# First expert pair gathered straight into its operand, low halves on GpSimd, gate/up weights in halves, last three pairs unpipelined, 32-bit down weights

## What is computed

```python
g_sel = argmax(x @ w_rg + b_rg)                 # one group of 4
e_prob = softmax(e_logits of that group)        # 8 experts
top_v, top_i = top_k(e_prob, 2)                 # two of them, weights normalised
h = silu(x @ w_gate[e]) * (x @ w_up[e])         # 1024 -> 256
y += (h * gate[e]) @ w_down[e]                  # 256 -> 1024
```

## Time and profile before

| | |
|---|---|
| median of 3 runs | 1422.86 us (1418.54 to 1423.76) |
| profiled execution | 1424.52 us, span 1423.2 us |
| PE busy | 1260.6 us (89%) |
| DVE busy | 713.2 us (50%) |
| ACT busy | 511.3 us (36%) |
| GpSimd busy | 141.6 us (10%) |
| moved by DMA | 340.32 MB, mean 239 GB/s |
| mean granted TensorE clock | 0.937 |

### The profile page before, as it was taken

The page is one execution under the profiler, slowest core; times in us unless marked ns, Lnnn a source line. Parts: engine busy times, 40 slices in busy tenths (PEclk is TensorE's granted clock), DMA queues, the critical chain, the costliest instruction groups (busy, mean ns, idle before and its releaser), DMA issues. The chain is left out here.

```text
span 1423.2 us, 21723 instructions
## 1 busy us (share of the span) xinstructions
PE 1260.6 (89%) x8724; PEld 791.9 (56%) x8724; DVE 713.2 (50%) x1273; ACT 511.3 (36%) x839; POOL 141.6 (10%) x185
## 2 busy tenths in 40 slices
PE   6799999989888789988989998969897969998885
PEld 5676678866665543433336766756664734333332
DVE  3655376655434514645465665436433451564553
ACT  3443323154332213343345333454432311433433
POOL 5100031110000101101001130000000101110100
PEclk9899998799998789999999998999998989999998
DMA  8464353357648049999973468503873616999992
GB/s 240 155 210 129 114 159 115 109 167 283 234 163 332 35 194 388 422 420 421 421 288 114 144 205 311 178 1 104 313 262 151 262 71 239 420 421 421 421 421 108
DMA packets 112835, 340.32 MB, mean 239 GB/s; under 512 B 7487, under 2 KB 75403, under 8 KB 84049
## 3 DMA queue, kind: packets, MB, share of 16 engines
q1 hardware_dynamic: 107296, 322.20, 60.4%
q0 software_dynamic: 4992, 15.47, 3.5%
q10 hardware_dynamic: 432, 1.11, 0.2%
HBM read 328.21 MB, written 10.54 MB: 238 GB/s over the span
## 5 line engine op out<-in xcount | busy, mean ns | idle before, releaser
L2151 PE MATMUL ps<-arena,mkv 128*64 128x512 f32 x1024 | 240.3, 623 | 36.6 <-DMA arena<-in_w_exp_up 27.6
L558 PE MATMUL ps<-bx,wh 128*128 128x320 f16 (+1 forms) x640 | 194.5, 304 | 32.8 <-DVE wl L552 10.6
L552 DVE SCALAR_TENSOR_TENSOR wl<-stg,wh 128x1024 f16<-128x1024 f32 x128 | 160.9, 1296 | 96.1 <-ACT wh L545 95.9
L559 PE MATMUL ps<-bx,wh 128*128 128x320 f16 (+1 forms) x640 | 194.4, 304 | 0.0
L560 PE MATMUL ps<-bx,wl 128*128 128x320 f16 (+1 forms) x640 | 194.1, 303 | 0.0
L545 ACT ACTIVATE wh<-stg 128x1024 f16<-128x1024 f32 x128 | 128.4, 1050 | 177.5 <-PE ps L560 154.5
L2151 PEld LDWEIGHTS ps<-arena,mkv 128*64 128x64 f32 x1024 | 87.4, 143 | 175.6 <-issue 175.2
L2367 DVE SCALAR_TENSOR_TENSOR wl<-arena,wh 128x1024 f16<-128x1024 f32 x56 | 67.6, 1248 | 63.9 <-ACT wh L2315 63.9
L558 PEld LDWEIGHTS ps<-bx,wh 128*128 128x128 f16 x640 | 64.9, 101 | 59.1 <-issue 27.5
L558 PE MATMUL ps<-arena,wh 128*128 128x320 f16 x288 | 88.3, 307 | 3.7 <-DVE arena L1381 3.0
L559 PE MATMUL ps<-arena,wh 128*128 128x320 f16 x288 | 88.2, 306 | 0.0
(11 more groups left out here) (440 smaller groups left out, 1962.7 us busy)
## 6 DMA issues: line engine op xcount, KB each, us to landing
arena<-in_w_exp_gate SPq DMA_DIRECT2D x64, 1024.0 KB, 15.0
arena<-in_w_exp_up SPq DMA_DIRECT2D x64, 1024.0 KB, 17.1
arena<-in_w_exp_down SPq DMA_DIRECT2D x32, 1024.0 KB, 19.8
stg<-in_w_exp_down SPq DMA_DIRECT2D x32, 1024.0 KB, 18.0
arena<-in_cache_mem_k SPq DMA_DIRECT2D x16, 1024.0 KB, 7.2
arena<-in_cache_mem_v SPq DMA_DIRECT2D x16, 1024.0 KB, 4.9
stg<-in_w_in_a SPq DMA_DIRECT2D x28, 512.0 KB, 4.7
stg<-in_w_qkv_c SPq DMA_DIRECT2D x20, 512.0 KB, 4.6
```

The source lines that it names most:

```text
L552: nc.vector.scalar_tensor_tensor(wl[:, s, c], src[:, c], WSCALE, wh[:, s, c], ALU.mult, ALU.subtract).then_inc(S["w_lo"], 1)
L558: nc.tensor.matmul(out, wh[:, s, at:at + 128], hi, start=start, stop=False)
L559: nc.tensor.matmul(out, wh[:, s, at:at + 128], lo, start=False, stop=False)
L2151: last = nc.tensor.matmul(ps[64 * j:64 * j + 64, UB, :], xe[:, q % 2, j, k, :], gu[:, g % 2, j, :, k, :], start=(k == 0), stop=(k == KD - ...
```

## The change

- A first gather of its own: `pk0` holds 64 columns for each of experts 0 and 1, made from the masked ranks `posw` (rank + 1 where the token goes to that expert, else 0), before slot numbers exist. `gather_first` (40 matmuls, k by k, behind all low halves) takes the place of `first_pe` and stands inside the If. ACT copies its two banks straight to `xe`, GpSimd's copies of pair 0 go. The ranks' maximum, the flag and `posw` come first on DVE.
- The low halves: ACT evicts each transposed block a second time in 32 bits (`xs`), and GpSimd (`route_pool`) subtracts the high part. The six instructions of DVE go.
- The general gather starts at slot 0: S1 = 256 slots in `gather_next`, now behind up(0), and 448 in `gather_rest`: two columns ahead of up(1), seven behind down(0, 1), ahead of up(2). Before it was three columns ahead of up(1) and six between weigh(1) and select(1).
- `load_up` issues eight DMAs of 512 KB, in two halves of k with a semaphore each. up(q) waits for each half where it needs it, and releases the first half behind k = 3, the second in weigh(q).
- HALVED is gone: all pairs use 32-bit down weights.
- Pairs 13 to 15 (behind TURN = 12) are not pipelined: up(q), weigh, select, combine(q-1), transpose_h(q), down(q, 0), down(q, 1).
- `seed` moves from behind down(0, 1) to behind select(2).

The core of the diff:

```diff
@@ load_up
-            if g >= 2:
-                sp.wait_ge(gu_used, g - 1)
-            for j in range(2):
-                for m, src in enumerate((w_gate_f, w_up_f)):
-                    sp.dma_start(gu[:, g % 2, j, m], src[2 * g + j]).then_inc(gu_in[g % 2], 16)
+            for h in range(2):
+                if g >= 2:
+                    sp.wait_ge(gu_used, 2 * (g - 2) + h + 1)
+                k = slice(4 * h, 4 * h + 4)
+                for j in range(2):
+                    for m, src in enumerate((w_gate_f, w_up_f)):
+                        sp.dma_start(gu[:, g % 2, j, m, k], src[2 * g + j][:, k]).then_inc(gu_in[g % 2][h], 16)
@@ route_act
-            nc.scalar.mul(dst, src, rtok[:, 1, g // 2:g // 2 + 1]).then_inc(S["xt_hi"], 1)
+            nc.scalar.mul(dst, src, rtok[:, 1, g // 2:g // 2 + 1])
+            nc.scalar.mul(xs[:, g], src, rtok[:, 1, g // 2:g // 2 + 1]).then_inc(S["xt_f32"], 1)
@@ route_dve
         dve.wait_ge(S["rank_ps"], l + 1)
+        link(V.reduce_max(cmax, ps[:, 7, 96:128], AX.X))
+        V.tensor_scalar(roff[0:1, NFIT:NFIT + 1], cmax[0:1, :], CAP + 0.5, None, ALU.is_le
+                        ).then_inc(S["off_ready"], 1)
+        link(V.scalar_tensor_tensor(posw[:], ps[:, 7, 0:96].rearrange("p (t n) -> p t n", t=3), 1.0, amat[:], ALU.add,
+                                    ALU.mult))
+        dve.wait_ge(S["rc_in"], 16 * (l + 1))
+        for i in range(3):
+            for j in range(2):
+                last = V.tensor_scalar(pk0[:, i, CAP * j:CAP * j + CAP], iota[:, 1:CAP + 1], posw[:, i, j:j + 1], None,
+                                       ALU.is_equal)
+        last.then_inc(S["pk_ready"], 1)
...
-        slots(slice(0, S0))
-        for g in range(6):
...
-            V.scalar_tensor_tensor(dst[rows], src[rows], rtok[rows, 1, i:i + 1], nat_part(g, xnh)[0][rows],
-                                   ALU.mult, ALU.subtract).then_inc(S["xt_lo"], 1)
+        slots(slice(0, S1))
...
+    def route_pool(pool, l):
+        for g in range(6):
+            rows, low = (slice(64, 128), xnh) if g >= 4 else (slice(0, 128), xnl)
+            hi = nat_part(g, xnh)[0]
+            pool.wait_ge(S["xt_f32"], 6 * l + g + 1)
+            if g >= 4:
+                pool.wait_ge(S["xt_lo"], 6 * l + g)
+            nc.gpsimd.tensor_tensor(nat_part(g, low)[0][rows], xs[rows, g], hi[rows], ALU.subtract
+                                    ).then_inc(S["xt_lo"], 1)
@@ moe_pe
+        gather_first()
+        up(0)
+        gather_gates()
+        gather_next()
+        weigh(0)
+        select(0)
+        transpose_h(0)
+        gather_rest(0, 2)
+        if rounds > 1:
+            gather_rest(2, KD + 1)
+        for q in range(1, TURN[rounds] + 1):
+            up(q)
+            weigh(q)
             select(q)
-            if q == 1:
+            if q == 2:
                 gathered()
+                if l == 1:
+                    seed()
             if q >= 2:
                 combine(q - 2)
             down(q - 1, 0)
             transpose_h(q)
             down(q - 1, 1)
-            if q == 1 and l == 1:
-                seed()
-        combine(last_step - 1)
-        down(last_step, 0)
-        down(last_step, 1)
+            if q == 1 and rounds == 1:
+                gather_rest(2, KD + 1)
+        q = TURN[rounds]
+        combine(q - 1)
+        down(q, 0)
+        down(q, 1)
+        for q in range(TURN[rounds] + 1, last_step + 1):
+            up(q)
+            weigh(q)
+            select(q)
+            combine(q - 1)
+            transpose_h(q)
+            down(q, 0)
+            down(q, 1)
         combine(last_step)
@@ moe_act
+        first_part(0)
+        first_part(1)
+        gate_half(0)
+        first_gates()
+        next_part()
+        to_hidden(0)
+        rest(0)
...
+        for q in range(TURN[rounds] + 1, last_step + 1):
+            y_high(q - 1, 0)
+            y_high(q - 1, 1)
+            gate_half(q)
+            to_hidden(q)
         if l == 0:
             for s in range(2):
                 split_hi(act, UNIT["qkv"][0] + s, s, arena[:, 2048 * s:2048 * s + 2048])
```

More of the change, by code:

```diff
@@ L25 @@
 NSLOT = 2 * T + CAP
-S0 = 128
-S1 = 2 * S0
+S1 = 256
 SR = NSLOT - S1
@@ L352, in build @@
     mem_in = [sem("mem_in0"), sem("mem_in1")]
-    gu_in = [sem("gu_in0"), sem("gu_in1")]
+    gu_in = [[sem(f"gu_in{n}{h}") for h in range(2)] for n in range(2)]
     dw_in = [sem("dw_in0"), sem("dw_in1")]
@@ L2109, in moe_pe, with gather_first @@
         last_step = NPAIR * rounds - 1
-        extra = 2 if rounds == 1 else 0
+        def gather_first():
+            pe.wait_ge(S["cleared"], 3 * l + 3)
+            pe.wait_ge(S["pk_ready"], 3 * l + 1)
+            pe.wait_ge(S["xt_lo"], 6 * l + 6)
+            for k in range(KD):
+                for n, (x, i) in enumerate(PARTS):
+                    last = nc.tensor.matmul(ps[:, k // 4, 128 * (k % 4):128 * (k % 4) + 128], x[:, i, k, :], pk0[:, i, :],
+                                            start=(n == 0 and k % 4 == 0), stop=(n == 4), skip_group_check=True)
+                if k % 4 == 3:
+                    last.then_inc(S["xg_ps"], 1)
@@ L2112, in gather_next, with gather_gates @@
+        def gather_gates():
+            pe.wait_ge(S["gate_lo"], l + 1)
+            for i, (t0, n) in enumerate(TILES):
+                last = nc.tensor.transpose(ps[0:NE, 2, t0:t0 + n], posw[0:n, i, :], ident[0:n, 0:n])
+            for n, (x, i) in enumerate(PARTS):
+                last = nc.tensor.matmul(ps[:, 2, 384:512], x[:, i, KD, :], pk0[:, i, :], start=(n == 0), stop=(n == 4))
+            last.then_inc(S["xg_ps"], 1)
         def gather_next():
-            pe.wait_ge(S["pk_ready"], 2 * l + 2)
+            pe.wait_ge(S["pk_ready"], 3 * l + 2)
@@ L2153, in up @@
                                             skip_group_check=True)
+                if k == 3 and q % rounds == rounds - 1:
+                    last.then_inc(gu_used, 1)
             last.then_inc(M["up_ps"], 1)
@@ L2317, in y_high @@
         def y_high(q, half):
             act.wait_ge(M["y_ps"], 2 * q + half + 1)
-            scale = 1 / WSCALE if rounds == 1 and q in HALVED else 1.0
-            nc.scalar.mul(yh[:, 512 * half:512 * half + 512], ps[:, (Y0, Y1)[half], :], scale).then_inc(M["y_hi"], 1)
-        if rounds > 1:
-            next_part()
-            rest(0, 2, 4, 6, 8)
-        for q in range(last_step + 1):
-            if rounds == 1 and q - 1 in HALVED:
-                halve(q - 1)
+            nc.scalar.copy(yh[:, 512 * half:512 * half + 512], ps[:, (Y0, Y1)[half], :]).then_inc(M["y_hi"], 1)
@@ L2328, in moe_act, with to_hidden @@
+        def to_hidden(q):
+            act.wait_ge(M["ht_ps"], q + 1)
+            nc.scalar.copy(hT[:, q % 2, :], ps[:, UB, 0:256]).then_inc(M["ht_ready"], 1)
+        first_part(0)
[5 more added lines that the diff above has]
+        rest(0)
+        if rounds > 1:
+            rest(2, 4, 6, 8)
+        for q in range(1, TURN[rounds] + 1):
             gate_half(q)
-            if rounds == 1 and q == 0:
-                next_part()
-                rest(0, 2)
+            y_high(q - 1, 0)
+            to_hidden(q)
+            y_high(q - 1, 1)
@@ L2376, in y_low, with hidden @@
             dve.wait_ge(M["y_hi"], 2 * q + half + 1)
-            halved = rounds == 1 and q in HALVED
-            if half == 1 and q % rounds == rounds - 1 and not halved:
+            if half == 1 and q % rounds == rounds - 1:
                 V.memset(cmax[0:1], 0.0).then_inc(dw_used, 1)
-            V.scalar_tensor_tensor(yl[:, f], ps[:, (Y0, Y1)[half], :], 1 / WSCALE if halved else 1.0, yh[:, f],
-                                   ALU.mult, ALU.subtract).then_inc(M["y_lo"], 1)
-        next_part()
-        rest(*((1, 3, 5, 7) if rounds > 1 else (1,)))
-        for q in range(last_step + 1):
-            if rounds == 1 and q - 1 in HALVED:
-                halve(q - 1, 0)
+            V.tensor_tensor(yl[:, f], ps[:, (Y0, Y1)[half], :], yh[:, f], ALU.subtract).then_inc(M["y_lo"], 1)
+        def hidden(q):
             dve.wait_ge(M["sel_ps"], q + 1)
@@ L2400, in moe_dve @@
             V.scalar_tensor_tensor(hg, ps[:, UB, 256:512], gcol, ab, ALU.mult, ALU.mult).then_inc(M["h_ready"], 1)
[L2401 to L2412 removed]
+        next_part()
+        hidden(0)
+        rest(1)
+        if rounds > 1:
+            rest(3, 5, 7)
+        for q in range(1, TURN[rounds] + 1):
+            hidden(q)
+            y_low(q - 1, 0)
+            y_low(q - 1, 1)
+            if rounds == 1 and q == 1:
+                rest(3, 5, 7)
+        for q in range(TURN[rounds] + 1, last_step + 1):
+            y_low(q - 1, 0)
+            y_low(q - 1, 1)
+            hidden(q)
         if l == 0:
```

282 lines of the change are left out of this document (82 added, 200 removed).

## The result

The changed kernel takes 1438.59 us (median of 4 runs, 1434.73 to 1445.82) against 1422.86 before: a ratio of 1.0123, 95% interval 1.0077 to 1.0168. It is 15.7 us slower; forecast were 5.7 us, 1428.5.

The account below looks back on a forecast made before the run. The weight stream (DMA) bounds the two MoE stages. Opening +1.0 and -0.5, steady part 0, tail +2.7 and +3.4 make +6.6 on 1424.5, less 1.7 (1429.4) and 1 for the flag's bound: 1428.5; range 1418 to 1439.

Parts of the forecast that it names:

- the steady part's term for the DMAs of 512 KB: Weight stream, steady pairs: 16 issues of 0.45 us for two pairs, nothing against 14.92 us a pair.
- (a) to (c), the lock: Router: ACT evicts twice, GpSimd subtracts; DVE's two-operand instructions wait for GpSimd, amat at 486 to 488, flag about 488.9.
- Rivals 1 and 2: Router: small DVE instructions don't wait for GpSimd, 1419.2 us, chance 0.22; or GpSimd's subtraction is the bound, 1439.6, chance 0.18.
- (d), (e), the jump and the first gather: Opening on PE: 3.8 us jump behind the flag, gather of 4.7 us, up(0) at 497.4 instead of 499.16, taking 7.1.
- (f) to (h), the rest of the opening: From up(0) to D3's issue: up(2) 1.4 us later, U4 0.4 earlier, D3 at 554.4 behind a 1.5 us hole.
- the forecast's +1.0 for the stream: Opening, layer 0: after the hole before D3 the weight stream ends 1.0 us later.
- The 32-bit down weights at 0: Steady pairs: PE's 13.51 us a pair stays under the stream's 14.92, so dropping the split weights costs 0.
- The releases for U15 and D15 still come 5 us or more early: Stage end: the last pair's weight buffers are freed at least 5 us early despite the unpipelined order.
- The tail: D14's landing to last combine, unpipelined: 22.2 us in layer 1 (+2.7), 24.3 in layer 0 (+3.4).
- The rivals: Besides the two on the router: PE becomes the bound, 1436, chance 0.05; halves bring more with a free tail, 1413, 0.05.

Follow-up runs that it names:

- e1_whole: Changed kernel with the gate/up weights again whole, in four 1-MB DMAs a pair (8-KB rows), released and waited for as a whole: 1431.75 us, ratio 1.0047.
- r5_before_halves: Kernel before with only the gate/up weights in eight 512-KB DMAs a pair, first half released behind k = 3: 1430.35 us, ratio 1.0053.
- e4_low_late: Changed kernel with one added wait: GpSimd starts its six subtractions only when DVE has written amat: 1428.32 us, ratio 1.0050.
- r6_before_32bit: Kernel before with only the down weights of all pairs kept 32-bit, so ACT's and DVE's splits go: 1423.48 us, ratio 1.0024.
- e3_pipelined: Changed kernel with the last three pairs pipelined again (TURN at the last step): 1421.41 us, ratio 0.9980.

## Why the prediction was wrong, point by point

The forecast was +5.7 us on the median, the result +15.7. By the stages: +6.6 forecast, +14.6 measured. The step that failed is the steady part's term for the DMAs of 512 KB, put at nothing: e1_whole and r5_before_halves show 6.9 and 6.7 us for the halves.

- **(a) to (c), the lock: right.** amat was to come at 486 to 488, so 9.95 to 11.95 us behind the router's start; it came at 9.96 in both layers. GpSimd's block was put at 1.26 us and took 1.16 to 1.22. Rivals 1 and 2 fell by these rows. e4_low_late shows that GpSimd is the cause: with it held back the same instructions take 0.18 us. By the rule of the Trainium skill quoted in the prediction (GPSIMD Engine Reference, section Specifications) instructions with two SBUF inputs contend with GpSimd; this trace agrees, down to 24 columns (six of seven waited), and the one-input reductions ran free.
- **(d), (e), the jump and the first gather: right.** The gather was forecast 16.7 us behind the router's start and came at 16.4 and 15.8; the jump took 4.8 us behind the flag instead of 3.8, from a flag 1.5 us earlier than forecast, so two misses cancelled in part. up(0) ended at 28.5, forecast 28.5, but took 7.75 us, not the 7.1 of the full clock.
- **(f) to (h), the rest of the opening: right to D3, partly by luck.** up(1) at 38.7 (forecast 38.6), up(2) at 59.6 behind 2.66 us for GpSimd's copy (forecast 61.7 behind 2.9), because up(1) ran at the full clock. D3 was issued at 75.8 (forecast 78.4), 1.1 us later than before (forecast 3.6). It landed 1.1 us later than before, the forecast's +1.0 for the stream, but by other terms: the issues of U4 and D3 were 2.0 and 2.6 us cheaper, and the slow restart, which had no term, took that back.
- **The steady part, "DMAs of 512 KB instead of 1 MB: nothing against 14.92": wrong.** I counted the issues and not the rows. 4-KB rows bring 412 GB/s where 8-KB rows bring 421. For the 12 pairs from U4 to U15, 75.5 MB, that is 183.3 against 179.3 us: an estimate of 4 us a layer. e1_whole gave 6.9 us back for both, r5_before_halves paid 6.7 for it; these hold the slow restart too, and what the halves gain elsewhere.
- **The 32-bit down weights at 0: right** (r6_before_32bit, 1423.5).
- **"The releases for U15 and D15 still come 5 us or more early": just right in time, and near the edge.** U15 went out at 716.19, 5.6 us before D13, the load ahead of it, had landed (721.80); in the kernel before it was 12.6 us. The dip behind it delayed D14 by some 0.6 us. The step left out the first unpipelined pair: down(12) waits for D12, which the queue brings behind U13, and up(13), whose buffer U15 needs, stands behind it.
- **The tail: right in size.** Forecast 22.2 us from D14 to layer 1's last combine and 24.3 in layer 0; from down(14)'s start it was 21.6 and 24.9. It was no measure of what the turn costs, since the pipelined end had become shorter too (e3_pipelined).
- **The rest of the sum.** Stages +14.6 = the forecast's +6.6, and 8 us by which D14 came later than forecast in the two layers (4.9 and 3.2, down(14)'s start against D14's landing before). By the landings in the traces, the nine pair steps from D5 to D14 took 137.4 and 138.4 us instead of 134.5 and 135.1: 6.2 us, of which 0.6 are the dip in layer 0 and some 5 the rate (nine steps of 15.2 against 14.92 in two layers). The other 1.9 us came between D3 and D5 of layer 0; D5 was 2.9 us later than before there, in e1_whole 0.6 us earlier.

The rivals all looked at the router and at PE; none had the stream's rate, though a diff that cuts a DMA's rows in half stood in the change. The tail's cost was seen, but not its cause, the order of the queue, so that 18 us stayed hidden behind a number that was right.

## What to carry to other kernels

Where a stage stands on DMA, price a change in the shape of a transfer by the stream's rate, not by its issues: 2% on 75 MB is 4 us. Look at how the stream restarts behind a gap as well. When the order of use is changed at the end of a stream, change the order of the loads with it, and count from the last landing only the work that needs that landing; the halves of the last load pay there, and no other place was found here where they do. Work moved to an engine off the path can hold up a chain of small instructions on another: start it behind the chain, and let it cover a jump that must be paid anyway.
